# A two-layer encoder trunk on one core: one-column sums, another order of VectorE's work after each FFN, and another order of the first `mla_out` products

## The reference, cut to what matters

```python
def rms_norm(x, g):
    xf = x.astype(jnp.float32)
    y = xf * lax.rsqrt(jnp.mean(xf * xf, axis=-1, keepdims=True) + EPS)
    return (y * g.astype(jnp.float32)).astype(x.dtype)

def swiglu_ffn(h, w_gate, w_up, w_down):
    return (jax.nn.silu(h @ w_gate) * (h @ w_up)) @ w_down

# layer 0: short gated convolution
x = x + short_conv_mixer(rms_norm(x, g), w_in, conv_w, w_out)
x = x + swiglu_ffn(rms_norm(x, g), w_gate, w_up, w_down)     # hidden width 2816
# layer 1: multi-head latent attention, 16 heads, chunk-causal mask
x = x + mla_mixer(rms_norm(x, g), ...)                        # ends in  o @ w_o
x = x + swiglu_ffn(rms_norm(x, g), w_gate, w_up, w_down)
out = rms_norm(x, final_norm_g)
```

## Time and profile before

| | |
|---|---|
| median of 3 runs | 1089.42 us (1088.82 to 1089.45) |
| the profiled execution | 1089.42 us, its span 1087.5 us |
| TensorE matmuls | 1074.9 us busy, 99% |
| VectorE | 808.6 us, 74% |
| ScalarE | 470.4 us, 43% |
| GpSimd | 226.0 us, 21% |
| waits of TensorE for `wgt_lo` | 1.4 us, two of them |

### The profile page before, as it was taken

One profiled execution on the slowest core, in us unless ns is written; L12 is line 12 of the kernel. 1 busy time (PEld: TensorE's weight loads), 2 busy tenths in 40 slices (PEclk: granted clock), 3 DMA queues, 4 the chain that ended last, 5 costly groups with the idle time before them and its releaser, 6 DMA issues. The chain is left out here.

```text
span 1087.5 us, 18730 instructions
## 1 busy us (share of the span) xinstructions
PE 1074.9 (99%) x6732; PEld 957.8 (88%) x6732; DVE 808.6 (74%) x1117; ACT 470.4 (43%) x698; POOL 226.0 (21%) x209
## 2 busy tenths in 40 slices
PE   8999999999999999999999999999999999999997
PEld 7888888999999998888888766789999999978887
DVE  5655659999999999444556678599999999984343
ACT  6222236544444456222347377465454444552222
POOL 6000001322322321111200245013332332101110
PEclk9999999999999999999999999999999999999999
DMA  7333242233233234333421202013233233332321
GB/s 199 96 96 116 79 114 78 78 117 105 88 116 116 83 100 120 107 94 99 126 72 48 58 20 59 22 56 117 79 115 116 87 106 116 106 106 81 106 66 78
DMA packets 144039, 101.68 MB, mean 93 GB/s; under 512 B 3912, under 2 KB 142336, under 8 KB 144000
## 3 DMA queue, kind: packets, MB, share of 16 engines
q1 hardware_dynamic: 143648, 100.61, 30.4%
q0 software_dynamic: 320, 0.55, 0.2%
q10 hardware_dynamic: 32, 0.01, 0.0%
HBM read 99.06 MB, written 2.10 MB: 93 GB/s over the span
## 5 line engine op out<-in xcount | busy, mean ns | idle before, releaser
L375 PE MATMUL ps<-x_op_hi,op_w_hi 128*128 128x256 f32 x1232 | 349.4, 284 | 0.2 <-DVE op_w_lo L541 0.2
L376 PE MATMUL ps<-x_op_lo,op_w_hi 128*128 128x256 f32 x1232 | 348.6, 283 | 0.0
L377 PE MATMUL ps<-x_op_hi,op_w_lo 128*128 128x256 f32 x1232 | 348.6, 283 | 0.0
L375 PEld LDWEIGHTS ps<-x_op_hi,op_w_hi 128*128 128x128 f32 x1232 | 236.4, 192 | 0.9 <-DVE op_w_lo L541 0.6
L376 PEld LDWEIGHTS ps<-x_op_lo,op_w_hi 128*128 128x128 f32 x1232 | 236.5, 192 | 0.1
L377 PEld LDWEIGHTS ps<-x_op_hi,op_w_lo 128*128 128x128 f32 x1232 | 236.5, 192 | 0.0
L375 PE MATMUL ps<-hid_hi,wgt_hi 128*128 128x512 f32 (+1 forms) x550 | 211.4, 384 | 1.4 <-DVE wgt_lo L359 1.4
L377 PE MATMUL ps<-hid_hi,wgt_lo 128*128 128x512 f32 (+1 forms) x550 | 209.5, 381 | 0.0
L376 PE MATMUL ps<-hid_lo,wgt_hi 128*128 128x512 f32 (+1 forms) x550 | 209.4, 381 | 0.0
L359 DVE TENSOR_TENSOR wgt_lo<-raw,wgt_hi 128x1024 fp32r<-128x1024 f32 (+4 forms) x131 | 138.0, 1071 | 90.2 <-ACT wgt_hi L350 88.9
L350 ACT ACTIVATE wgt_hi<-raw 128x1024 fp32r<-128x1024 f32 (+4 forms) x131 | 106.8, 831 | 144.2 <-PE ps L377 142.3
(11 more groups left out here) (167 smaller groups left out, 1238.6 us busy)
## 6 DMA issues: line engine op xcount, KB each, us to landing
pair_raw<-in_ffn_w_gate SPq DMA_DIRECT2D x22, 1024.0 KB, 5.4
pair_raw<-in_ffn_w_up SPq DMA_DIRECT2D x22, 1024.0 KB, 5.4
raw<-in_conv_w_in SPq DMA_DIRECT2D x24, 512.0 KB, 3.8
raw<-in_ffn_w_down SPq DMA_DIRECT2D x32, 384.0 KB, 3.6
raw<-in_ffn_w_down SPq DMA_DIRECT2D x32, 320.0 KB, 2.9
raw<-in_conv_w_out SPq DMA_DIRECT2D x8, 512.0 KB, 3.8
raw<-in_mla_w_o SPq DMA_DIRECT2D x8, 512.0 KB, 3.8
x_nat<-in_x SPq DMA_DIRECT2D x4, 512.0 KB, 6.9
```

The costliest lines, as they stand in the source:

```text
L375: nc.tensor.matmul(acc, wh, xh, start=first, stop=False)
L376: nc.tensor.matmul(acc, wh, xl, start=False, stop=False)
L377: return nc.tensor.matmul(acc, wl, xh, start=False, stop=last)
```

## The change

There are three edits. `column_sums` takes one column of `ones` and writes one column for each block, and its two readers read four adjacent columns. VectorE's last group makes weight unit 2 of the down projection ahead of `hidden_lo(3)`, leaves 4 and 5 for after the group, and makes unit 3 just ahead of `hidden_lo(10)`. TensorE does chunks 0 to 5 of unit 0 ahead of `turn(15)`, puts chunk 6 and the seven early chunks of unit 1 ahead of `weigh(7)`, the seven of unit 2 behind it, and then the late chunk of units 0, 1 and 2.

```diff
             for t in range(TB):
                 for n, part in enumerate(parts):
-                    ins = nc.tensor.matmul(ps[:, STAT_BANK, t * P:(t + 1) * P], part[:, t * P:(t + 1) * P], ones[:, :],
+                    ins = nc.tensor.matmul(ps[:, STAT_BANK, t:t + 1], part[:, t * P:(t + 1) * P], ones[:, 0:1],
                                            start=n == 0, stop=n == len(parts) - 1)
...
-            nc.scalar.activation(root_c, ps[:, STAT_BANK, 0:S:P], ACT.Sqrt, scale=1.0 / width,
+            nc.scalar.activation(root_c, ps[:, STAT_BANK, 0:TB], ACT.Sqrt, scale=1.0 / width,
...
+                    weights(2)
                     if nxt is None:
-                        for q in range(3, 6):
-                            hidden_lo(q)
-                    else:
-                        weights(2)
+                        hidden_lo(3)
                     wait(ve, op_used, op0 + 7)
...
-                hidden_lo(6)
-                unit_lo(ve, f"down{l}", 0, 2)
-                hidden_lo(7)
-                hidden_lo(8)
-                unit_lo(ve, f"down{l}", 0, 3)
-                for q in range(9, PAIRS_F):
+                for q in range(4, PAIRS_F):
+                    if q == PAIRS_F - 1:
+                        unit_lo(ve, f"down{l}", 0, 3)
                     hidden_lo(q)
...
-                nc.vector.tensor_tensor(ms_c, ps[:, STAT_BANK, 0:S:P], inv_in2, ALU.mult).then_inc(ms_done, 1)
+                nc.vector.tensor_tensor(ms_c, ps[:, STAT_BANK, 0:TB], inv_in2, ALU.mult).then_inc(ms_done, 1)
...
             pe.wait_ge(s_read, 3 * HEADS)
-            mla_out_products(0, [0, 1])
+            mla_out_products(0, list(range(6)))
             turn(HEADS - 1)
-            mla_out_products(0, [2, 3, 4])
+            mla_out_products(0, [6])
+            mla_out_products(1, early)
             weigh(PAIRS - 1)
-            mla_out_products(0, [5, 6])
-            mla_out_products(1, [0, 1])
-            mla_out_products(0, late)
-            mla_out_products(1, every[2:])
-            mla_out_products(2, every)
+            mla_out_products(2, early)
+            for u in range(3):
+                mla_out_products(u, late)
             pe.wait_ge(pt_front, HEADS)
             mla_out_products(3, every)
```

## The result

The changed kernel takes 1096.26 us (median of 5 runs, 1094.07 to 1097.8) against 1089.42 (1088.82 to 1089.69): a ratio of 1.0061 [1.005, 1.0072], 6.8 us slower. The forecast was 1094.3 us, the range 1091.6 to 1096.4. The runs scatter over 3.7 us, those of the kernel before over 0.9, and the time goes with the mean granted clock of TensorE: over 30 executions, the four at 0.992 took 1097.78 to 1097.85 us, and the four at 0.998 took 1094.07 to 1094.90.

A forecast was written before the change was run, and what follows sets the result against it. The prediction took TensorE, busy 99% of the span, as the bound. Its terms for the three edits, 0 + 1.25 + 3.7 = 4.95 us, added to 1089.42 gave 1094.3 us, with a range of 1091.6 to 1096.4.

The forecast's parts named there:

- mechanisms of edits 2 and 3: Down projections: late `hidden_lo(4)` stalls chunk 8, net 1.25 us slower; `mla_out`: late unit 0 delays VectorE, 3.7 us slower.
- edit 1's price of 0: Sums in `column_sums`: one column instead of 128 changes TensorE's time by 0, since the stationary tile loads stay.
- the forecast's own range: Whole kernel: 1091.8 to 1095.8 us, from adding 1.5 + 0.9 and 4.8 + 1.6 to 1089.42.
- edit 3's pause: `seven_product` 0 after `mla_out`: TensorE stands about 3 us waiting for block 6.
- the two rows of starts in the earlier trace: TensorE's timeline: eight wide sum records take 0.82 us, eight one-column records 0.81, deciding for no change.
- the isolated gap by columns: Sums in `column_sums`: matmul distance follows the columns, 31 ns off each of 72 records, 2.2 us saved.
- above, 0: Sums in `column_sums`: upper bound of the one-column price, 0; the lower bound was 3.8 us gained.
- The chain of the prediction: `mla_out`: first residual at 700.3, 32.4 us for blocks 0 to 6, block 7 at 732.7, product 4 3.7 us later.
- The case that the lateness is absorbed: `mla_out`, VectorE's blocks 0 to 6: if they need at most 28.6 us, no cost there; 1090.7 us, chance 0.10.
- The clock rival: `seven_product` 0: a pause of some 3 us drops the granted clock, 2 us more, 1096.3 us; chance 0.12.

The follow-up runs named there:

- e2_order: Only VectorE's order after each FFN's last group changed as in the change, against the kernel before: 1090.47 us, 1.04 us slower.
- e3_products: Only the order of `mla_out`'s first products changed as in the change, against the kernel before: 1093.25 us, 3.82 us slower.
- e4_wide: The changed kernel with all sums back at 128 columns, against the kernel before: 1094.78 us, 5.35 us slower.
- e1_sums: Only `column_sums` and its two readers changed to one column, against the kernel before: 1089.81 us, ratio 1.0006.
- e6_all_but_first: The kernel before with one-column sums everywhere except in the first norm: 1089.06 us, ratio 1.0002.
- e5_first_only: The kernel before with one-column sums in the first norm alone: 1090.32 us, ratio 1.001.
- e11_first_no_wait: The kernel before with a one-column first-norm sum alone and one more `conv_in` chunk ahead of it: 1088.67 us, ratio 0.9995.
- e8_order2: The kernel before with weight unit 2 ahead of the adds, but `hidden_lo` 4, 5 and 6 kept ahead of it: 1088.62 us, ratio 0.9997.
- e7_lead: The kernel before with the new `mla_out` product order, but unit 0's late chunk after 18 chunks instead of 22: 1090.32 us, 1.34 us slower.
- e9_after_first_wide: The changed kernel with 128 columns in the first norm's sum alone: 1095.17 us, against the changed kernel's 1096.26.

## Why the prediction was right, and the term it mis-sized

The direction holds, and so do the mechanisms of edits 2 and 3; edit 1's price of 0 does not. The number is in part luck. 1096.26 is above the forecast's own range (1091.8 to 1095.8) and inside the whole range by 0.14 us, and that range reached so high only for a clock that falls in edit 3's pause. About half of the excess over 1094.3 comes from another place, the first norm's sum. Of the 7.6 us by which the span of the changed kernel's profile is longer (1095.1 against 1087.5), the shift between equal instructions of the two traces gives the parts (7.7 together; small differences elsewhere give 0.1 back):

| where | us | predicted |
|---|---|---|
| up to the first sum, its start 24.98 against 24.43 (input DMAs and `gain`) | 0.55 | none |
| clock behind the first sum, edit 1 | 1.6 | 0 |
| down projection, layer 0, edit 2 | 0.85 | 0.64 |
| `mla_out` to product 4, edit 3 | 3.70 | 3.7 |
| second group of that FFN, wait for `op_w_lo` | 0.37 | none |
| down projection, layer 1, edit 2 | 0.64 | 0.61 (1.25 less 0.64) |

Two of these lines belong to no edit, as far as the runs show. The wait for `op_w_lo` is 0.2 us before and 0.6 in the changed kernel, but it is absent in `e2_order`, `e3_products` and `e4_wide`, so it comes and goes from one profile to the next. And in every other profile that has the first sum in its old place it starts 0.2 to 0.7 us later than in the profile of the kernel before.

**Edit 1.** TensorE's time for the sum is the same 1.78 us with 16 records of 128 columns as of one, as the two rows of starts in the earlier trace rows had said. The Trainium skill (TensorE: Matmul & The Clock Gate, Back-to-back issue gap) also says that in a stream of weight loads and matmuls the spacing is set by both. That fits the trace, where each record has its load and the width changes nothing; the isolated gap by columns, which would have saved 2.2 us, does not hold here.

What failed is the end of the step, "So I take 0", with "above, 0" as its upper bound: only TensorE's time was priced, not what the sum does to the clock. It was 0.4 us in the median of `e1_sums`, which is not clear of the scatter, and 1.6 to 1.8 us between the two groups of executions. Three runs tie this to one place. `e6_all_but_first` has no second group, `e5_first_only` has, and in `e11_first_no_wait` the group goes away with the wait ahead of the sum, though the columns stay at one. With 128 columns the wait for `gain` does no harm either: `e2_order` has it (0.3 us) and is in one group, and `e4_wide` has it with 0.6 us and no fall behind it in its profile. So, as far as these runs tell, it takes both, TensorE waiting for `gain` and one-column matmuls right behind the wait. (The extra chunk of `e11_first_no_wait` also puts the sum one chunk later in the stream, which these runs don't separate from the wait's end.) The fall itself was profiled in the changed kernel alone; in `e1_sums` and `e5_first_only` the profiles are of the lower group, and that their upper group is the same fall is argued from its size and the mean clock (one of the lower executions of `e5_first_only` also reads 0.997).

**Edit 2.** The mechanism is as worked out: no wait at chunk 12, a stall at chunk 8 because `hidden_lo(4)` stands behind unit 2, `hidden_lo(3)`, both adds and the product, and a small one at chunk 17. The stall in layer 0 is 1.40 against 1.30. The whole edit is 1.04 us by itself against 1.25, and the shifts in the profile of `e2_order` are 0.60 in layer 0 and 0.45 in layer 1. `e8_order2` shows the other side of it: the same move of unit 2 with `hidden_lo(4)` kept ahead costs nothing.

**Edit 3.** 3.82 us alone against 3.7. The chain of the prediction can be read off step by step: residual at 700.3, 32.3 us for the blocks, block 7 at 732.6 (732.7), the pause of 2.84 ("about 3 us"), product 4 later by 3.70 (3.7), and by 3.71 in the profile of `e3_products`. `e7_lead` confirms it by a change of size: 2.7 us of lead given back are 2.5 us of time. The case that the lateness is absorbed is out.

**The clock rival** (0.12) named the right danger for edit 3's pause, and it is real in part of the executions. It is in the profiles of `e4_wide` and `e9_after_first_wide`, and not in those of `e3_products` and of the changed kernel. The Trainium skill (TensorE: Matmul & The Clock Gate, HAM oscillation) says that pauses between bursts can take the array back to the lower level; the traces of `e4_wide` and `e9_after_first_wide` agree, with a pause of 2.84 us. Its price is not the 2 us put on it, though, but 0.9 us in both profiles that have it, because the slow stretch uses up the wait at product 4. In `e3_products` the upper executions are also 0.9 us longer; that this is the same fall is not shown by a profile. The first norm has at least as large a part in the excess: `e9_after_first_wide` takes 0.9 to 1.1 us off the median without touching the pause.

**The sum.** The parts alone add up to 0.4 + 1.04 + 3.82 = 5.3 us, and the whole is 6.8. Executions of the changed kernel with the highest mean clock, 0.998, take 1094.1 to 1094.9, where the forecast of 1094.3 lies; the rest of them put the median 2 us higher. What stays open is the executions at 1097.8: their mean clock of 0.992 is 0.006 below the best, which at half speed is 0.006 x 1095 / 0.5 = 13 us more at the lower level. The stretch at the end differs by some 3 us between profiles, so this is some three or four stretches of 3.4 us (an estimate). Two places are known, and they cost 1.6 + 0.9 = 2.5 of the 2.9 to 3.7 us. The last sum is a third, but a small one: in the profile of `e9_after_first_wide` the clock falls at 1086.80, between its matmuls, and that costs 0.26 us. Where the others lie no profile shows, since none was taken of such an execution, and the execution of `e4_wide` at 1096.09 and 0.994 says that such stretches don't need one-column sums. It is also open how often each of the two known falls comes in the changed kernel, since its one profile shows the first alone.

## What to carry to other kernels

Before moving something ahead in a producer's queue, or finishing units in one batch instead of one by one, write down for each item behind it when its consumer needs it: both reorderings here made an item late that the profile had shown no wait for, because it had been on time. Where a chain of work hangs on the first finished unit, its length (32 us for seven blocks here) sets how late that unit may be. And if the executions of a kernel fall into groups, look at each one's mean granted clock before looking for a wait: an edit that saves TensorE nothing can still cost a stretch at half speed.

## What the runs showed of the hardware

- A wait of 0.49 us followed by 16 records of one column (1.78 us) was enough for the granted clock to fall to 1.2 GHz in the changed kernel, about 1.1 us after the sum's end and for 3.4 us, while matmuls of 512 columns ran without a hole. With 128 columns the sum takes the same 1.78 us, and no fall was seen behind it.
- The fall is not certain: going by the groups of executions, it comes in five of eleven in `e1_sums` and six of eleven in `e5_first_only`. A pause of 2.84 us dropped the clock in two of the four profiles that have it unfilled.
- In all three profiled falls with matmuls behind them (changed kernel, `e4_wide`, `e9_after_first_wide`) the clock is back after about 3.4 us.
- How soon a fall comes differs: behind the same pause it came 0.2 us after TensorE started again in `e4_wide` and 1.3 us after in `e9_after_first_wide`.
